# Dense expert products of a PEER mixer in plain float32, on fewer token tiles

## The reference, cut to what matters

```
s1, i1 = lax.top_k(s[:, :, 0], 16)          # 128 first keys
s2, i2 = lax.top_k(s[:, :, 1], 16)          # 128 second keys
sc, pos = lax.top_k(cand, 16)               # 16 x 16 sums
gw = jax.nn.softmax(sc, axis=-1)
a = einsum('thkd,td->thk', u_tab[eidx], hb) # eidx = 128*i1 + i2
w = gelu(a) * gw
out = einsum('thk,thkd->td', w, v_tab[eidx])
```

## Time and profile before

| | PE | DVE | ACT | POOL |
|---|---|---|---|---|
| busy us | 4832.2 | 4022.5 | 2138.3 | 2372.2 |
| share of the span | 84% | 70% | 37% | 41% |

### The profile page before, as it was taken

One profiled execution on the slowest core, in us unless ns is written; L12 is line 12 of the kernel. 1 busy time (PEld: TensorE's weight loads), 2 busy tenths in 40 slices (PEclk: granted clock), 3 DMA queues, 4 the chain that ended last, 5 costly groups with the idle time before them and its releaser, 6 DMA issues. The chain is left out here.

```text
span 5734.3 us, 72971 instructions
## 1 busy us (share of the span) xinstructions
PE 4832.2 (84%) x27874; PEld 4064.5 (71%) x27874; DVE 4022.5 (70%) x6929; ACT 2138.3 (37%) x3263; POOL 2372.2 (41%) x1488
## 2 busy tenths in 40 slices
PE   6975888899999997888886875777888999978887
PEld 5844876778888885666665543335788998978887
DVE  3146753199888874999997247983388774089997
ACT  2124222155555553222222144442355555522222
POOL 0001320056554664777772002440165553366663
PEclk8988988999999998999998887888899999989998
DMA  4111012267776897999994001112376675398884
GB/s 153 55 61 63 5 30 74 105 230 258 254 235 226 299 319 276 316 322 313 323 319 138 32 1 43 48 41 81 129 258 235 228 249 182 118 318 283 283 283 160
DMA packets 487495, 1052.48 MB, mean 184 GB/s; under 512 B 44758, under 2 KB 261580, under 8 KB 480492
## 3 DMA queue, kind: packets, MB, share of 16 engines
q1 hardware_dynamic: 372112, 636.63, 32.7%
q0 software_dynamic: 110592, 402.70, 20.6%
q10 hardware_dynamic: 4444, 8.48, 0.4%
HBM read 911.36 MB, written 136.31 MB: 183 GB/s over the span
## 5 line engine op out<-in xcount | busy, mean ns | idle before, releaser
L1522 POOL TENSOR_TENSOR u_lo<-u_raw,u_hi 128x1024 fp32r<-128x1024 f32 x256 | 630.5, 2463 | 1361.9 <-ACT u_hi L1627 1361.6
L1953 PE MATMUL banks<-w_hi,v_hi 128*128 128x512 f32 (+1 forms) x2048 | 778.8, 380 | 235.7 <-DVE w_lo L1979 173.4
L1570 PE MATMUL banks<-h_hi,ut_hi 128*128 128x512 f32 (+1 forms) x2048 | 796.6, 389 | 0.0
L1914 POOL TENSOR_TENSOR v_lo<-v_raw,v_hi 128x1024 fp32r<-128x1024 f32 x256 | 613.5, 2397 | 359.7 <-ACT v_hi L1930 358.0
L1953 PE MATMUL banks<-w_lo,v_hi 128*128 128x512 f32 (+1 forms) x2048 | 758.9, 371 | 0.0
L1570 PE MATMUL banks<-h_lo,ut_hi 128*128 128x512 f32 (+1 forms) x2048 | 758.6, 370 | 0.0
L1953 PE MATMUL banks<-w_hi,v_lo 128*128 128x512 f32 (+1 forms) x2048 | 758.2, 370 | 0.0
L1570 PE MATMUL banks<-h_hi,ut_lo 128*128 128x512 f32 (+1 forms) x2048 | 757.7, 370 | 0.0
L1953 PEld LDWEIGHTS banks<-w_hi,v_hi 128*128 128x128 f32 x2048 | 395.3, 193 | 344.3 <-POOL v_lo L1914 149.7
L1824 DVE CUSTOM_DVE_ANT_0 rows<-rows,banks 128x1024 f32<-128x1024 f32 x384 | 462.4, 1211 | 96.9 <-DMA rows<-peer_u,expert 80.4
L1905 POOL DMA_INDIRECT v_fetched<-peer_v,expert x384 | 427.5, 1113 | 142.7 <-DVE banks L2003 80.8
(11 more groups left out here) (415 smaller groups left out, 9715.5 us busy)
## 6 DMA issues: line engine op xcount, KB each, us to landing
u_raw<-peer_u SPq DMA_DIRECT2D x256, 512.0 KB, 5.3
v_raw<-peer_v SPq DMA_DIRECT2D x256, 512.0 KB, 5.3
gate_table<-part SPq DMA_DIRECT2D x28, 2048.0 KB, 8.4
activations<-acts SPq DMA_DIRECT2D x128, 256.0 KB, 4.2
acts_in<-activations SPq DMA_DIRECT2D x128, 256.0 KB, 4.4
gates<-gate_table SPq DMA_DIRECT2D x32, 1024.0 KB, 11.6
activations<-acts SPq DMA_DIRECT2D x128, 192.0 KB, 2.3
acts_in<-activations SPq DMA_DIRECT2D x128, 192.0 KB, 4.2
```

Source lines behind the costliest of these rows:

```text
L1522: nc.gpsimd.tensor_tensor(u_lo[:, i % 2], u_raw[:, i % 2], u_hi[:, i % 2].bitcast(F32), ALU.subtract)\
L1570: last = nc.tensor.matmul(out, u[:, i % 2, k * P:(k + 1) * P], h[:, k, 0:ND], start=(k == 0 and u is ut_hi and h is hi), stop=(k == DK - 1 ...
L1914: nc.gpsimd.tensor_tensor(v_lo[:, i % 2, r], v_raw[:, r], v_hi[:, i % 2, r].bitcast(F32), ALU.subtract)\
L1953: last = nc.tensor.matmul(out, v[:, i % 2, r, m * P:(m + 1) * P], w[:, i % 2, r], start=(r == 0 and v is v_hi and w is w_hi), stop=(r == G ...
```

## The change

Rounded parts and remainders go. The products take float32 operands as they are, and the dense tiles are three of six and two of four.

- Activate: `u_raw` is turned by 8 float32 transposes a tile, copied out by two copies into `u_t`, and multiplied by 8 products; VectorE first adds `hi` and `lo` of the dense tokens into one buffer `h_dense`. `round_u` and `low` are gone; GpSimd only issues gathers, with no order against the expert tiles. `HOTS` is 4. `Turns` has new costs, an order of routing with three fetched tiles, and spreads the quads over all fetched rows.
- Mix: v rows and activations go to TensorE as loaded, from eight buffers each (two groups), freed by `y_done`; the gathers' ring has 16 slots. ScalarE only copies `y_tok`. Where the sums of all channel blocks fit four banks (layer 1: 8 x 256 columns, `RESIDENT`), they stay there over all 128 tiles and are added once at the end; in layer 0 (8 x 384) they are added per group as before.

```diff
-RING = 8
-DENSE_TILES = (4, 3)
+RING = 16
+DENSE_TILES = (3, 2)
...
-TB, QUAD, HOTS, GROUP, ACT_ROWS = 32, 4, 2, 4, 5
+TB, QUAD, HOTS, GROUP = 32, 4, 4, 4
+U_RING, V_RING, V_ROWS = 8, 16, 8
...
-        self.tile_us = 1.4 + 24 * dense * P * 0.000443 + 1.1 * self.quads / KEYS
-        self.first, self.step = 52, 1.6 if self.fetched == 2 else 1.0
+        self.tile_us = 1.25 + 8 * dense * P * 0.0017 + 1.2 * self.quads / KEYS
+        self.first = 52
+        self.step = (self.rows - self.first - 4) / self.quads
...
-        return 60 + 1.4 * min(row, self.rows) + 1.9 * steps + 2.0 * self.quads_before(row)
+        return 60 + 1.33 * min(row, self.rows) + 1.75 * steps + 1.5 * self.quads_before(row)
...
                 if i >= 2:
-                    sp.wait_ge(u_lo_ready, i - 1)
+                    sp.wait_ge(turned, 2 * (i - 2) + 2)
...
-            for i in range(KEYS):
-                if i + 2 < KEYS:
-                    low(i + 2)
-                while s < plan.rows and plan.expert_tile(s - 4) <= i:
-                    fetch(s)
-                    s += 1
+            for s in range(plan.rows):
+                fetch(s)
...
-                    for u, h in ((ut_hi, hi), (ut_hi, lo), (ut_lo, hi)):
-                        last = nc.tensor.matmul(out, u[:, i % 2, k * P:(k + 1) * P], h[:, k, 0:ND],
+                    last = nc.tensor.matmul(out, u_t[:, i % 2, k * P:(k + 1) * P], h[:, k], start=(k == 0),
+                                            stop=(k == DK - 1))
...
+    RESIDENT = ND * DK <= BANKS * BANK
...
+            for j in range(KEYS):
+                i, r = divmod(j, GROUP)
+                if r == 0 and j >= V_ROWS:
+                    sp.wait_ge(y_done, groups_done(i - V_ROWS // GROUP + 1))
...
+                if RESIDENT:
+                    for j in range(i * GROUP, (i + 1) * GROUP):
+                        ready(j)
+                        for m in range(DK):
+                            last = product(j, m, j == 0 and m * ND % BANK == 0,
+                                           j == KEYS - 1 and (m + 1) * ND % BANK == 0)
                     last.then_inc(y_done, 1)
+                else:
+                    for m in range(DK):
+                        u = i * DK + m
+                        if u >= BANKS:
+                            pe.wait_ge(y_added, u - BANKS + 1)
+                        for r in range(GROUP):
+                            if m == 0:
+                                ready(i * GROUP + r)
+                            last = product(i * GROUP + r, m, r == 0, r == GROUP - 1)
+                        last.then_inc(y_done, 1)
...
-                        if m < GROUP:
-                            multiply((i + 1) * GROUP + m)
-                        else:
-                            low((i + 1) * GROUP + m - GROUP)
-                    if u:
+                    if i + 1 < GROUPS and m % 2 == 0:
+                        multiply((i + 1) * GROUP + m // 2)
+                    if u and not RESIDENT:
                         add(u - 1)
```

More of the change, by code:

```diff
@@ L1552, in turn @@
                 if half == 0:
[L1553 to L1560, removed]
+                    pe.wait_ge(u_loaded[i % 2], 16 * (i // 2 + 1))
+                if i:
+                    pe.wait_ge(ut_ready, 2 * i + half - 1)
+                for k in range(HALF):
+                    c = (half * HALF + k) * P
+                    last = nc.tensor.transpose(ps[:, TURN + c:TURN + c + P], u_raw[:, i % 2, c:c + P], g.ident[:])
                 last.then_inc(turned, 1)
@@ L1900, in _ @@
         def _(pool):
-            def fetch(s):
-                if s >= RING:
-                    pool.wait_ge(consumed, s - RING + 1)
+            for s in range(plan.rows):
+                if s >= V_RING:
+                    pool.wait_ge(consumed, s - V_RING + 1)
                 t = s // SLOTS
                 pool.indirect_dma_start(
-                    out=ring[:, s % RING, :], out_offset=None, in_=rows_of_v,
+                    out=ring[:, s % V_RING, :], out_offset=None, in_=rows_of_v,
@@ L1907, in fetch @@
                     in_offset=bass.IndirectOffsetOnAxis(ap=expert[:, t, s % SLOTS:s % SLOTS + 1], axis=0))\
-                    .then_inc(fetched[s % RING], 16)
-            s = 0
-            for j in range(KEYS):
-                i, r = divmod(j, GROUP)
-                pool.wait_ge(v_hi_ready, j + 1)
-                nc.gpsimd.tensor_tensor(v_lo[:, i % 2, r], v_raw[:, r], v_hi[:, i % 2, r].bitcast(F32), ALU.subtract)\
-                    .then_inc(v_lo_ready, 1)
-                while s < plan.rows and s < (j - 3) * PER // GROUP + RING - 2:
-                    fetch(s)
-                    s += 1
@@ L1919, in _ @@
-            while s < plan.rows:
-                fetch(s)
-                s += 1
+                    .then_inc(fetched[s % V_RING], 16)
         @block.scalar
         def _(act):
-            for j in range(KEYS):
-                i, r = divmod(j, GROUP)
-                act.wait_ge(v_loaded[r], 16 * (i + 1))
-                if r == 0 and i >= 2:
-                    act.wait_ge(y_done, (i - 1) * DK)
-                nc.scalar.copy(v_hi[:, i % 2, r], v_raw[:, r]).then_inc(v_hi_ready, 1)
-                act.wait_ge(weighted, j + 1)
-                nc.scalar.copy(w_hi[:, i % 2, r], acts[:, j % ACT_ROWS]).then_inc(w_hi_ready, 1)
-                for t in range(NG - 1):
-                    if i == (t + 1) * GROUPS // NG and r == GROUP - 1:
-                        act.wait_ge(consumed, (t + 1) * SLOTS)
-                        nc.scalar.copy(y_tok[:, t], acc(0)).then_inc(half_kept, 1)
@@ L1937, in _ @@
-            act.wait_ge(consumed, NG * SLOTS)
-            nc.scalar.copy(y_tok[:, NG - 1], acc(0)).then_inc(half_kept, 1)
+            for t in range(NG):
+                act.wait_ge(consumed, (t + 1) * SLOTS)
+                nc.scalar.copy(y_tok[:, t], acc(0)).then_inc(half_kept, 1)
         @block.tensor
         def _(pe):
-            for i in range(GROUPS):
-                for m in range(DK):
-                    u = i * DK + m
-                    if u >= BANKS:
-                        pe.wait_ge(y_added, u - BANKS + 1)
-                    out = ps[:, u % BANKS * BANK:u % BANKS * BANK + ND]
-                    for r in range(GROUP):
-                        if m == 0:
-                            pe.wait_ge(v_lo_ready, i * GROUP + r + 1)
-                            pe.wait_ge(w_lo_ready, i * GROUP + r + 1)
-                        for v, w in ((v_hi, w_hi), (v_hi, w_lo), (v_lo, w_hi)):
-                            last = nc.tensor.matmul(out, v[:, i % 2, r, m * P:(m + 1) * P], w[:, i % 2, r],
-                                                    start=(r == 0 and v is v_hi and w is w_hi),
-                                                    stop=(r == GROUP - 1 and v is v_lo))
-                    last.then_inc(y_done, 1)
@@ L1995, in weighted_row @@
                     dve.wait_ge(summed, t)
[L1996 to L1997 removed]
+                row = ring[:, s % V_RING, :]
+                dve.wait_ge(fetched[s % V_RING], 16 * (rounds[s % V_RING] + s // V_RING + 1))
                 if s >= 2:
@@ L2008, in _ @@
                 multiply(r)
-            for r in range(GROUP):
-                low(r)
             dve.wait_ge(x_loaded, 16)
```

158 lines of the change are left out of this document (66 added, 92 removed).

## The result

The kernel after takes 5492.65 us (median of 4 runs, 5486.16 to 5505.47), the kernel before 5750.32 beside it: a ratio of 0.9556, 95% interval 0.9537 to 0.9575, or 258 us less. The forecast was 156 less, 5596. The profiled execution has a span of 5484.3 us.

| stage | before | forecast | after | forecast change | change |
|---|---|---|---|---|---|
| activate, layer 0 | 1084.0 | 1054 | 987.7 | -30 | -96 |
| mix, layer 0 | 882.3 | 918 | 961.1 | +36 | +79 |
| activate, layer 1 | 910.5 | 746 | 716.8 | -165 | -194 |
| mix, layer 1 | 683.5 | 687 | 637.4 | +3 | -46 |
| all the rest | 2174 | 2174 | 2181.4 | 0 | +7 |

What follows compares the result with a forecast made beforehand. TensorE was taken to bound the activate stages and VectorE the mix stages, with DMA the new bound; -30 + 36 - 165 + 3 = -156 us gave 5580, or 5596 against the median of runs, range 5450 to 5750.

Steps and rivals of the forecast that it cites:

- the likeliest case: Four DMA-bound stretches at net 340 to 380 GB/s, kernel 5510 to 5700 us; chance 0.55.
- rival 1: Activate and mix: full queues run at 390 GB/s for good, 2% idle, kernel 5436 us; chance 0.15.
- 190 to 280: Activate stages: TensorE loses 190 to 280 us in each and stops being the end of it.
- the price read from one overlapping pair in the earlier trace: Mix: a gate multiply took 2.86 us, ending with GpSimd's subtraction, where 0.68 would do.
- the rate of full queues: DMA-bound stretches of the four stages: 849.2 MB in 2377 us, 357 GB/s; gain used up at 335 GB/s.
- the cost of the added wait: Mix layer 0: SyncE waits for `y_done` before loading a group; VectorE stands 1 to 3 us a group, slack 7.
- The DMA engines lose nothing: Mix: gathers, 16 deep, go on during the added `y_done` wait, so DMA loses no time.
- under 335 GB/s: Mix stages: a rate below this shows the prediction wrong; the gain is used up at 335 GB/s.
- Rival 4: Activate: written order and u's two buffers make TensorE late with quads, 60 us a stage, kernel 5716; chance 0.07.
- TensorE is the last releaser: Any of the four activate and mix stages: TensorE releasing last would show the prediction wrong.
- Rivals 2 and 3: Rival 2 (0.10): old packet times at 92% share, 5904; rival 3 (0.04): TensorE's clock stays low in mix layer 1, 5789.

## Why the prediction came out as it did

**How near it was.** The measured 5492.65 is inside the stated range and 103 us under the forecast. It is also under the 5510 to 5700 of the likeliest case. (That case's 340 to 380 GB/s are not those times: 849.2 MB at 380 take 2235 us, which gives 5454; and rival 1's third stage adds up to 723, not 719.)

**Right: what leaves and what comes next.** TensorE no longer holds the activate stages but for the end of layer 1's, and did not get the mix ones. Its busy time in activate fell by 140 and 192 us; the forecast's "190 to 280" sets its new busy time against the old length of the stage. The paces held: 47 records of 384 columns in 15.32 us are 0.326 each (0.329 forecast), the multiply is 0.55 us at 384 columns and 0.42 at 256, VectorE's work 665 and 364 us (680 and 356 forecast). In activate of layer 0 the waits for quads (88.0 us in the earlier trace rows) are gone from VectorE's list and 42.0 us for gathers stand there. The experiment with idle GpSimd confirms the price read from one overlapping pair in the earlier trace rows, and that the mix stages before paid it.

**Mis-sized: the rate of full queues.** The likeliest case took 450, 897, 360 and 670 us for 849.2 MB, 357 GB/s. Measured: 2121.88 + 1.21 - 1710.93 = 412 us for the last 224 rows, 961 - 21 = 940, 4775.35 + 1.21 - 4453.14 = 323, and 637 - 17 = 620: 2295 us, 370 GB/s. The term failed in the three stretches where little else stood in the way: 390, 398 and 384 GB/s by the forecast's own bytes, which is rival 1's rate. It had the rows for it (302 to 533 GB/s in the earlier trace rows) and leaned on the packet times of the earlier trace rows as well, from queues that waited for other engines. Packets took longer there: 3.10 us a MB for gathers became 2.50. That is 38 us of the 66 by which activate of layer 0 beat its forecast, and most of the mix of layer 1 (rival 1 gave 639, measured 637.4).

The Trainium skill's "DMA: Bandwidth & Descriptors", section "Where 436 GB/s comes from", puts the HBM side at about 358 GB/s a core; by that estimate these bytes take 2372 us, no less. The runs don't agree: 2295 us in all, and 407 GB/s over 350 us on one core, against its 358. The Trainium skill's "HBM Reference", "Specifications (TRN2)", keeps that figure for two cores that stream at once and gives some 425 for one that streams alone; the trace is nearer to that, at 407.

**Failed: the cost of the added wait.** "VectorE may stand 1 to 3 us a group, which is inside its slack." It stood 262.3 / 32 = 8.2 us a group, above the slack of 7. Both sides of the comparison were off: the forecast gave 8 us from the wait to the first multiply against 6 to 8 us for the data to land, and measured are 4.1 and 12.5. The landing was taken from a DMA system with slack; on a full one the issue alone took up to 5.4 us. With VectorE's own 665 us, its 262 for activations and 31 for `x_t` make up the stage: it never stood for gathers, and the chain of request, landing and multiply set the pace of a group. "The DMA engines lose nothing" failed with it, though not while VectorE stood (376 GB/s): they lost in the second half of the way to the next request, when SyncE's queue had run dry (313 GB/s). With the request a group earlier the middle of the stage ran at 392 in place of 346. Undoing it gave 97 us (961.0 to 864.1, where rival 1 had 863). So +79 in this stage is the full rate's -18 and 97 for the wait. The depth of the gathers, the other suspect, was worth 8.

Such a wait in the list is not a price by itself: in the mix of layer 1 VectorE stands 228 us for activations too, at 393 GB/s, and the earlier request changed nothing there (637.4 to 636.8). By the prediction's own sign, mix "under 335 GB/s", layer 0 was on the line: 335 over the whole stage.

**Rival 4 was true in one stage.** u's two buffers did hold activate of layer 1, by 31 us, not 60; in layer 0 by nothing that can be told. Halving the products gave 17.6 in layer 1, so it was the loads' turn-round more than TensorE's work. The forecast allowed 10 us for the end of that stage, it was 4812.0 - 4776.6 = 35; in layer 0, 3. VectorE's last wait in layer 1 ends behind ScalarE and TensorE's last tiles, so "TensorE is the last releaser", a sign of being wrong, did come there. The first rows also went faster than forecast: 504 against 521 us in layer 0, 290 against 304 in layer 1.

**Rivals 2 and 3 did not come.** The granted clock was 0.88 in both mix stages, and VectorE waited for TensorE's banks 2.9 us in layer 0. With half the products gone it was 0.82 in activate of layer 0, and the stage was as long.

The errors partly cancelled: +43 us in one stage against 66, 29 and 50 in the other three. One thing the forecast did not say is that neither half of the change pays alone (+164 and +137 us, together -258). With four and three dense tiles float32 only lengthens TensorE's chain; with three and two, split products hold the gathers behind GpSimd's other work in activate, and VectorE is the bound in the mix of layer 1. Nor did it see that taking GpSimd's subtractions away, with nothing else changed, was worth 286 us.

What stays open: why the gathers' packets took 2.81 us a MB in the mix of layer 0 and 2.56 after the early request. The slow ones (2.9, against 2.6 while VectorE stands) lie between the waits, as much in the first halves as in the second, so an empty other queue is not the whole reason. Nor was it tried whether other tile counts beat three and two once the requests are early.

## What to carry to other kernels

Take the rate of a new DMA bound from slices where every queue is full, not from packet times of a stretch that another engine paced; read GB/s beside the share. Then look at every request that the change moves later, and give its data the landing time of a full system, 9 to 15 us here, not that of the old profile: asking a group earlier was worth 97 us. Look also at whether a queue runs dry between two requests. Tensor work on GpSimd is paid twice, by VectorE's operations on SBUF and by the gathers queued behind it.

## What the runs showed of the hardware that was not expected

- One core held 407 GB/s for 350 us, 70% of it 4 KB rows gathered by index, and 392 to 393 GB/s over 530 to 700 us with smaller rows beside them.
- A DMA share of 0.97 stood beside 346 GB/s, and one of 0.97 to 1.04 beside 382 to 407.
- With the queues full, an issue of activations on SyncE stood 5.44 us before the engine could go on.
- With SyncE's queue nearly empty and the ring of gathers 16 deep, the DMA engines moved 313 GB/s at a share of 0.92; with a ring of 8 it was 318 at 0.92.
- GpSimd's 128 x 1024 subtractions made VectorE's operations on two SBUF inputs 1.7 to 2.6 times as long (685 to 1173 and 694 to 1834 ns) and left the one with a PSUM operand alone (1273 and 1279 ns).
